# Adding the routed rows of a mixture of experts in memory instead of on chip, on one core

## What is computed

```python
e_id = g_idx * 8 + top_i            # best of 4 groups, then the best 2 of its 8 experts
h = silu(xi @ w_gate[e]) * (xi @ w_up[e])
yb = h @ w_down[e]                  # for each routed token of expert e, 1024 -> 512 -> 1024
ff = zeros.at[token].add(yb * weight)
y = LayerNorm(alpha * x1 + ff)
```

## Time and profile before

| | |
|---|---|
| median of three runs | 1056.05 us |
| time of the profiled execution | 1056.94 us |
| its span, first to last instruction | 1055.1 us |
| TensorE busy | 913.1 us, 87% |
| VectorE busy | 419.8 us, 40% |
| ScalarE busy | 283.8 us, 27% |
| GpSimd busy | 128.2 us, 12% |
| DMA | 264.77 MB, mean 251 GB/s |
| memory read and written | 258.98 MB and 15.16 MB |
| mean granted clock of TensorE | 0.955 |

### The profile page before, as it was taken

The page is one execution under the profiler, slowest core; times in us unless marked ns, Lnnn a source line. Parts: engine busy times, 40 slices in busy tenths (PEclk is TensorE's granted clock), DMA queues, the critical chain, the costliest instruction groups (busy, mean ns, idle before and its releaser), DMA issues.

```text
span 1055.1 us, 14518 instructions
## 1 busy us (share of the span) xinstructions
PE 913.1 (87%) x5905; PEld 625.0 (59%) x5905; DVE 419.8 (40%) x874; ACT 283.8 (27%) x531; POOL 128.2 (12%) x206
## 2 busy tenths in 40 slices
PE   4999999899999999999469999978777878778772
PEld 4989998898999989998433333323323323322220
DVE  3765867675656444532632112111111111111176
ACT  3667544444353422111401111101101101101121
POOL 2000300000000010030221211111111111100003
PEclk8999999889999999999769999999999999999975
DMA  9214722112212423265699999999999999999842
GB/s 286 96 54 89 190 84 70 59 41 81 81 42 80 87 81 81 80 263 217 240 391 426 420 422 423 422 420 425 423 421 423 423 421 423 423 421 423 338 165 81
DMA packets 86604, 264.77 MB, mean 251 GB/s; under 512 B 29291, under 2 KB 60151, under 8 KB 66026
## 3 DMA queue, kind: packets, MB, share of 16 engines
q1 hardware_dynamic: 79498, 248.56, 60.7%
q0 software_dynamic: 7040, 15.28, 3.9%
HBM read 258.98 MB, written 15.16 MB: 260 GB/s over the span
## 4 chain that ended last, share of the span: by engine, by line
PE 51%; SPq 19%; DMA 13%; DVE 11%; ACT 2%; issue 2%; POOL 1%; DVEq 0%; POOLq 0%; ACTq 0%
PE ps L782 29%; SPq L505 16%; DMA slot<-in_w_up 9%; PE ps L1078 9%; PE ps L1103 4%; SPq L508 3%; DMA raw<-in_w_o 2%; PE ps L908 1%; PE ps L874 1%; PE ps L898 1%; DMA st<-in_state_lru_h 1%; DVE hL L1535 1%; PE ps L1062 1%; DVE rawL L1454 1%; POOL zT L658 1%
## 5 line engine op out<-in xcount | busy, mean ns | idle before, releaser
L1078 PE MATMUL ps<-slot,xt 128*64 128x512 f32 x512 | 232.6, 601 | 40.3 <-DMA slot<-in_w_up 38.1
L1079 PE MATMUL ps<-slot,xt 128*64 128x512 f32 x512 | 233.2, 602 | 0.0
L1078 PEld LDWEIGHTS ps<-slot,xt 128*64 128x64 f32 x512 | 66.4, 138 | 177.8 <-issue 131.2
L782 PE MATMUL ps<-xTh,wh 128*128 128x260 f32 x704 | 147.7, 292 | 0.0
L782 PE MATMUL ps<-xTl,wh 128*128 128x260 f32 x704 | 143.9, 287 | 0.0
L782 PE MATMUL ps<-xTh,rawL 128*128 128x260 f32 x704 | 143.7, 286 | 0.0
L1103 PE MATMUL ps<-slot,hT 128*64 128x512 f32 x512 | 116.9, 597 | 29.2 <-issue 27.8
L1934 DVE TENSOR_TENSOR xt<-ps,g 128x512 f32<-128x512 f32 x32 | 22.1, 692 | 249.6 <-PE ps L1062 249.6
L1454 DVE TENSOR_TENSOR rawL<-raw,wh 128x1024 fp32r<-128x1024 f32 x68 | 84.1, 1241 | 87.1 <-ACT wh L1178 87.0
L782 PEld LDWEIGHTS ps<-xTh,wh 128*128 128x128 f32 x704 | 110.8, 193 | 5.9 <-issue 5.1
L782 PEld LDWEIGHTS ps<-xTl,wh 128*128 128x128 f32 x704 | 111.0, 193 | 0.0
(11 more groups left out here) (323 smaller groups left out, 1246.0 us busy)
## 6 DMA issues: line engine op xcount, KB each, us to landing
slot<-in_w_gate SPq DMA_DIRECT2D x64, 1024.0 KB, 29.8
slot<-in_w_up SPq DMA_DIRECT2D x64, 1024.0 KB, 32.1
slot<-in_w_down SPq DMA_DIRECT2D x32, 2048.0 KB, 33.3
raw<-in_w_in SPq DMA_DIRECT2D x18, 1024.0 KB, 5.2
raw<-in_w_in SPq DMA_DIRECT2D x16, 256.0 KB, 4.3
raw<-in_w_lru_out SPq DMA_DIRECT2D x4, 1024.0 KB, 4.8
raw<-in_w_attn_out SPq DMA_DIRECT2D x16, 256.0 KB, 4.5
raw<-in_w_o SPq DMA_DIRECT2D x4, 1024.0 KB, 5.1
```

The lines of the kernel that those rows point to most:

```text
L782: last = mm(out_of[:, a, 0:HT], w[:, k, :], x[:, k, a * HT:(a + 1) * HT], start=(k == 0 and n == 0), stop=(k == KT - 1 and n == 2))
L1078: mm(out[0:CAP, :], tokens, w[:, q, :], start=start, stop=stop)
L1079: last = mm(out[CAP:P, :], tokens, w[:, 4 + q, :], start=start, stop=stop)
```

## The change

`ff_half` shrinks to half: one row for each token. Both choices of a token have the same index, and a scatter adds to what the row holds instead of writing it. For that the buffer is cleared early from a memset tile, by two DMAs on GpSimd's queue before the window stores; the first scatter waits for them. Since a token's two rows are added by two different scatters, scatter e waits until scatter e-1 has landed (before: e-2). SP waits for the last scatter and loads one copy; the additions on VectorE and TensorE go, and VectorE adds the residual straight from the loaded rows in all five tiles.

```diff
+        zero = at("zero", [104, 256], F32, oE + 3072)
...
-        f1 = [at(f"f1{n}", [P, D], F32, 4096 * (TT + n)) for n in range(TT)]
...
-        ff_half = nc.dram_tensor("ff_half", [4 * T, 512], F32, kind="Internal").ap()
+        ff_half = nc.dram_tensor("ff_half", [2 * T, 512], F32, kind="Internal").ap()
...
-            for e in (NE - 2, NE - 1):
-                sp.wait_ge(*stored(e))
+            sp.wait_ge(*stored(NE - 1))
             for n in ORDER:
-                sp.dma_start(f0[n][0:ROWS[n], :], rows(ff_rows[0], n)).then_inc(s_x[n], 16)
-                sp.dma_start(f1[n][0:ROWS[n], :], rows(ff_rows[1], n)).then_inc(s_x[n], 16)
+                sp.dma_start(f0[n][0:ROWS[n], :], rows(ff_rows, n)).then_inc(s_x[n], 16)
...
+            link(gp.memset(zero[:, :], 0.0))
             pool.wait_ge(s_kva, 1)
+            for h in range(2):
+                pool.dma_start(ff_half[:, h * 256:(h + 1) * 256].rearrange("(a p) n -> p a n", a=10),
+                               zero[:, :].rearrange("p (a n) -> p a n", a=1).to_broadcast([104, 10, 256])).then_inc(s_ffz, 16)
...
-                gp.iota(tokv[:, n, :, 0:1], [[2 * T * n, 2], [0, 1]], base=2 * (T - P) - FARAWAY, channel_multiplier=2,
+                gp.iota(tokv[:, n, :, 0:1], [[0, 2], [0, 1]], base=2 * (T - P) - FARAWAY, channel_multiplier=2,
...
                 pool.indirect_dma_start(out=ff_half, out_offset=bass.IndirectOffsetOnAxis(ap=index[:, 0:1], axis=0),
-                                        in_=src[:, :], in_offset=None,
-                                        bounds_check=4 * T - 1, oob_is_err=False).then_inc(signal, 16)
+                                        in_=src[:, :], in_offset=None, compute_op=ALU.add,
+                                        bounds_check=2 * T - 1, oob_is_err=False).then_inc(signal, 16)
...
             def scatter(e):
                 j = e % 2
-                if e >= 2:
-                    pool.wait_ge(*stored(e - 2))
-                elif e == 0:
+                if e:
+                    pool.wait_ge(*stored(e - 1))
+                else:
                     pool.wait_ge(s_tabc, 3)
+                    pool.wait_ge(s_ffz, 32)
...
-            for m, n in enumerate(ORDER):
-                r = ROWS[n]
-                if m < 2:
-                    continue
-                pe.wait_ge(s_x[n], 48)
-                if m == 2:
-                    pe.wait_ge(s_ye, NE)
-                    pe.wait_ge(s_l2, 68)
-                if m == 4:
-                    pe.wait_ge(s_z, TT + 3)
-                for h in range(2):
-                    for k, f in enumerate((f0, f1)):
-                        last = mm(pair[m % 2][0:r, h, :], ident[0:r, 0:r], f[n][0:r, h * 512:(h + 1) * 512], start=(k == 0), stop=(k == 1))
-                last.then_inc(s_mix, 1)
...
-                if m >= 2:
-                    dve.wait_ge(s_mix, m + 3)
-                    rows_sum = flat[m % 2][0:r, :]
-                else:
-                    dve.wait_ge(s_x[n], 48)
-                    link(v.tensor_tensor(f0[n][0:r, :], f0[n][0:r, :], f1[n][0:r, :], ALU.add))
-                    rows_sum = f0[n][0:r, :]
+                dve.wait_ge(s_x[n], 32)
+                rows_sum = f0[n][0:r, :]
```

More of the change, by code:

```diff
@@ L304, in build @@
         x1_half = nc.dram_tensor("x1_half", [2 * T, 512], F32, kind="Internal").ap()
-        ff_half = nc.dram_tensor("ff_half", [4 * T, 512], F32, kind="Internal").ap()
+        ff_half = nc.dram_tensor("ff_half", [2 * T, 512], F32, kind="Internal").ap()
         x1_rows = x1_half.rearrange("(t h) n -> t (h n)", h=2)
-        ff_rows = ff_half.rearrange("(k t h) n -> k t (h n)", k=2, h=2)
+        ff_rows = ff_half.rearrange("(t h) n -> t (h n)", h=2)
         s_vec, s_st, s_wg, s_snk, s_snr = sem("vec_loaded"), sem("state_loaded"), sem("gate_w_loaded"), sem("sinks_loaded"), sem("row_sinks_loaded")
@@ L357, in build @@
         s_wx = [sem(f"chunk_loaded{n}") for n in range(RING)]
+        s_ffz = sem("ff_cleared")
         s_ig, s_id = sem("gather_index"), sem("scatter_index")
@@ L670, in _ @@
             for n in range(2):
-                gp.iota(tokv[:, n, :, 0:1], [[2 * T * n, 2], [0, 1]], base=2 * (T - P) - FARAWAY, channel_multiplier=2,
+                gp.iota(tokv[:, n, :, 0:1], [[0, 2], [0, 1]], base=2 * (T - P) - FARAWAY, channel_multiplier=2,
                         allow_small_or_imprecise_dtypes=True)
-                ins = gp.iota(tokv[:, n, :, 1:TT], [[2 * T * n, 2], [2 * P, TT - 1]], base=-FARAWAY, channel_multiplier=2,
+                ins = gp.iota(tokv[:, n, :, 1:TT], [[0, 2], [2 * P, TT - 1]], base=-FARAWAY, channel_multiplier=2,
                               allow_small_or_imprecise_dtypes=True)
@@ L740, in _ @@
             with pool.If(n_over > 0):
-                for e in (NE - 2, NE - 1):
-                    pool.wait_ge(*stored(e))
+                pool.wait_ge(*stored(NE - 1))
                 pool.sem_inc(s_ov["free"], 1)
```

## The result

The changed kernel takes 1076.68 us in the median of four runs (1076.31 to 1077.08), the kernel before 1056.49 us: a ratio of 1.0187 on record, 95% interval 1.0174 to 1.02. By the medians it is slower by 20.2 us; 11.35 were forecast, and the time lies in the stated range (1058 to 1082). The profiled execution took 1076.75 us, its span 1075.0.

A forecast was written before the change was run, and what follows sets the result against it. DMA transfers, unbroken from about 540 to 988 us, were taken to bound the expert loop, with a VectorE-set tail behind. 1056.94 - 2.45 + 13.8 = 1068.3, less 0.89: 1067.4 us; range 1058 to 1082.

The forecast's parts named there:

- The bound: Expert loop, about 540 to 988 us: DMA transfers never pause, so added DMA time moves the loop's end by as much.
- the add that is charged: Expert loop: each adding scatter must first read its target rows, 0.46 us for each of 30 scatters, +13.8 us.
- byte price: Expert loop: the added read charged by its bytes at 423 GB/s, 0.315 us a scatter, 9.4 us for 30.
- The clear at no cost: GpSimd's early queue: a memset and two DMAs delay later transfers by 18 us at most, covered by slack, costing nothing.
- the sample's cache transposes later than 168 us: Early part: a sign that would show the prediction wrong, meaning the clear's delay is not covered.
- The serial wait: Expert loop: waiting for scatter e-1 instead of e-2 gives a 9.05 us round, under the 15.74 us step: hidden.
- The second rival: Expert loop: waiting for each landing becomes the bound, above 14.54 us a round; +20.3 us, 1073.9 us; chance 0.16.
- The first rival: Expert loop: the adding scatter's read is free, leaving only the tail's 2.45 us gain, 1053.6 us; chance 0.11.
- The tail: After the expert loop: VectorE no longer adds f1 to f0 for tiles 0 and 1, -2.45 us.
- Nothing to gain there: Tail, tiles 2 to 4: TensorE's additions end before VectorE is free, and VectorE reads PSUM as fast as SBUF.
- memory reads rise by about 2 MB net: Whole kernel, a sign of being right: 4.26 MB of reads added by scatters, 2.13 fewer in the tail.
- another rival: Expert loop: the serial wait as bound, chance 0.16; its 15.0 us round, +28.0 us, set the range's upper end, 1082.

The follow-up runs named there:

- kernel with the clear early: The changed kernel with only its two clearing DMAs moved to a quiet stretch, issued at 50.16 instead of 116.60 us: 1065.78 us, 1.0083 of the kernel before.
- The add alone: The kernel before, with two copies, overlapping scatters and old tail, but every scatter adding and both copies cleared early: 1066.5 us, 1.0089 of before.
- no-add kernel: The changed kernel with clearing DMAs moved early and plain scatters instead of adding ones, still one at a time: 1055.13 us, 0.9982 of the kernel before.
- adding load in the tail: The kernel before, with VectorE's additions for tiles 0 and 1 replaced by GpSimd-issued DMAs adding the second copy in SBUF: 1054.62 us, 0.9979 of before.

## Why the prediction was right, and where it was not

**The bound, and the add that is charged: right.** The expert loop ends when the DMA engines are through, and the adding scatters lengthen it although the bytes counted did not grow. The term was +13.8, 0.46 us a scatter between a byte price of 0.315 and a gather's 0.61; measured over nine kernels it is 11.3 / 30 = 0.38 us, nearer to the bytes. The Trainium skill's rule ("Collectives: The Full Stack", "The bandwidth ceiling: the fold count and why AG ≠ RS ≠ AR") is that an add needs two source reads. The traces fit it in size, 9.4 us by it as an estimate and 11.3 measured; the second read itself shows only as packets.

**The clear at no cost: wrong, by 11 us.** "So some 2 us on GpSimd and, behind each other, 16 us on its queue. Queued behind them are the window stores, cK, cV and the conv stores". That list was of GpSimd's queue alone, and it came out: cK landed late without harm. What was left out is SP's queue. Its loads run on the same sixteen engines, and one of them, issued 1.2 us after the first clear, had to be in before TensorE ran out of work 16 us later. Two things make up the 11 us: TensorE stood for some 9 us, and by the number of its matmuls (15 and 26 from 142 to 150, where 35 in 4 us are usual) the lower clock cost some 2 more, an estimate. The prediction had named the sign, the sample's cache transposes later than 168 us, and they began at 178.8, but for another reason than the cache. Without this step the forecast would have met the kernel with the clear early: 1067.4 against 1065.8.

**The serial wait: right.** A round is landing plus overhead; 10.4 + 1.05 is 11.45, under the 14.54 from which it would decide. The second rival falls: GpSimd waits for landings, 214 us in all, but ScalarE's output comes last in 30 of the 32 rounds. The add alone, without the wait, has a loop only 0.5 us shorter.

**The first rival: refuted.** The add is not free. The Trainium skill's statement that the engines' limit lies at the SBUF ports ("DMA: Bandwidth & Descriptors", "Where 436 GB/s comes from"), taken strictly, would have left the loop at 455 us; the kernels with the add have 466.

**The tail: right but for a detail.** From the first step on x1 to the end of the span it was 1055.1 - 1008.33 = 46.77 us and is 1075.0 - 1030.44 = 44.56: 2.2 of the 2.45. That VectorE reads as fast from PSUM as from SBUF ("Nothing to gain there") was true of VectorE, but GpSimd paid: three of its four last additions, beside steps that now read both inputs from SBUF, take 3.2 us (1059.75), where they took 2.35 in the kernel before, so an output buffer comes free late and VectorE's last step waits for a store (1062.98, 1065.69). The other 1.1 us of the 3.3 lie before x1, where TensorE's products with the norm vectors took 3.64 us against 4.95. The stretches of these products, before and after:

```profile
1002.20:1007.20 5.00, 5.00 (x11) 2.22 (x10) 0.00 (x0) 1.71 (x2) 0.99 (x1) 0.72 0.08 28
```

```profile
1025.60:1029.30 3.70, 3.70 (x11) 1.74 (x10) 0.00 (x0) 1.71 (x2) 0.96 (x2) 1.00 0.03 6
```

The granted clock was 0.72 in one and 1.00 in the other. The change to the tail does not explain it: the add alone, with the old tail, has 3.64 us too. But all four kernels with adding scatters and the no-add kernel have 3.64, the other four 4.06 to 4.95, so another part of the change may have to do with it; that stays open.

**A sign that failed.** "memory reads rise by about 2 MB net": the page has 256.85 MB, 2.13 fewer than before. If the adding scatters read their rows, those 4.26 MB are not in its count, nor in the rate. They show only in the engines' time and in the packets.

That the time came within the range was luck: a missing term of 11.2 us met a loop term that was 1.8 us too large and a tail that gained 0.8 us more than forecast, and the range had been widened to 1082 for another rival.

## What to carry to other kernels

Price an add in memory as a second read at least: here, with the DMA engines as the bound, it cost 0.38 us a scatter against 0.315 for the bytes of that read, and only the engines' time and the packets said so. Put adding transfers where the engines have room, as the adding load in the tail does. Before a bulk transfer is put into a quiet-looking stretch, go through every queue that shares the engines and look for the load with the least time to spare: 2 MB cost 11 us at 116 us and about 1 us at most at 50 or 125. Take a change with three parts apart by stage and by part before judging it: here the tail's gain was real, and was to be had without the other two.

## What the runs showed that was not expected

One late load stopped the whole projection: landing 23.7 us against a longest of 5.2 before, 11 us for the kernel. TensorE also came back at a granted clock of 0.50, the lower of its two levels (1.2 GHz against 2.4), after it had done nothing from 134 to some 143; it read 0.67 from 146 to 150 and 1.00 after.

Moving work to idle GpSimd lost time: two additions that took VectorE 2.45 us made two of its other steps 2.0 us longer each. The Trainium skill, in "SBUF — State Buffer", section "Who interferes with whom", says that a VectorE instruction with two SBUF inputs contends with a GpSimd instruction that reads SBUF, and that one with at most one SBUF input does not, outside VectorE's two-port modes. Both traces agree: VectorE's 1.23 became 3.25 us, and GpSimd's 2.35 became 3.2 us once VectorE read both inputs from SBUF. GpSimd's row in the kernel before:

```profile
1035.58 2.35 POOL L767 TENSOR_TENSOR yout<-z,norms 128x1024 f32<-128x1024 f32 x1 [2.19 <-DVE z L2007]
```
